# Decoder block in float32 on one core: attention outputs in token rows scaled behind the product, gate row and mask in the single-pass format, delta rule with its products grouped by shape

## The reference, cut to what matters

```
# first attention, 16 heads of 64, query blocks of 128 (k up to the block's end)
s = q @ k.T * scale + logf_cum[q] - logf_cum[k]        # "gate row"
s = where(q >= k, s, -inf)                             # mask
o = softmax(s) @ v
# second attention, 8 heads: all 256 tokens lie in one block
l = q @ k.T * scale + rel_bias[bucket(q - k)]; masked; o = softmax(l) @ v
# delta rule, 8 heads of 64, chunks of 64 tokens
decay = exp(where(causal, g_cum[i] - g_cum[j], -inf))
m     = where(strict, (k * beta) @ k.T * decay, 0)
uw    = triangular_solve(m + eye, [v * beta, k * beta * exp(g_cum)])
a     = (q @ k.T) * decay                              # attn_intra
for each chunk:
    v_new = u - w @ state
    o     = q_dec @ state + a @ v_new
    state = state * g_last + k_dec.T @ v_new
o = o * rsqrt(mean(o * o) + eps) * norm_w * silu(z)
# then [o_att, o_gdn] @ w_out
```

## Time and profile before

| | |
|---|---|
| Runs | median 1853.99 us of 3 (1853.04 to 1855.04) |
| Profiled execution | 1854.81 us, span 1852.7 us |
| Mean granted clock of PE | 0.956 |
| PE busy | 1752.1 us (95%) |
| DVE busy | 1285.6 us (69%) |
| ACT busy | 989.5 us (53%) |
| First attention, first transpose of probabilities to first output projection | 440.42 to 487.21 us |
| Second attention, to the first transpose of the delta rule | 1455.0 to 1485.39 us |
| Delta rule, to the first product of the output projection | 1485.39 to 1626.61 us |

### The profile page before, as it was taken

The page is one execution under the profiler, slowest core; times in us unless marked ns, Lnnn a source line. Parts: engine busy times, 40 slices in busy tenths (PEclk is TensorE's granted clock), DMA queues, the critical chain, the costliest instruction groups (busy, mean ns, idle before and its releaser), DMA issues. The chain is left out here.

```text
span 1852.7 us, 24961 instructions
## 1 busy us (share of the span) xinstructions
PE 1752.1 (95%) x9866; PEld 1521.5 (82%) x9866; DVE 1285.6 (69%) x1366; ACT 989.5 (53%) x1077; POOL 15.9 (1%) x21
## 2 busy tenths in 40 slices
PE   6988999899989999999999999999879898989998
PEld 5857999797778888788888888888779688969997
DVE  4954544545379888989888888989775727565554
ACT  3334334454367777767777777777545221244443
POOL 1000000000000000000000000000010000000000
PEclk9999999899979999999999999999989968889999
DMA  6405554342139898989898998989843100034550
GB/s 259 148 17 193 193 189 159 137 182 92 46 133 363 316 371 330 353 333 359 319 372 330 358 365 322 365 326 368 326 152 137 46 1 1 1 136 161 197 188 23
DMA packets 31190, 401.50 MB, mean 217 GB/s; under 512 B 3688, under 2 KB 3952, under 8 KB 5520
## 3 DMA queue, kind: packets, MB, share of 16 engines
q1 hardware_dynamic: 30704, 399.44, 57.2%
q0 software_dynamic: 416, 1.06, 0.2%
HBM read 399.43 MB, written 1.06 MB: 216 GB/s over the span
## 5 line engine op out<-in xcount | busy, mean ns | idle before, releaser
L860 DVE TENSOR_TENSOR wl<-raw,wh 128x2048 fp32r<-128x2048 f32 x266 | 607.9, 2291 | 91.8 <-ACT wh L855 88.5
L855 ACT ACTIVATE wh<-raw 128x2048 fp32r<-128x2048 f32 x264 | 506.4, 1919 | 201.6 <-PE ps L1793 90.9
L1791 PE MATMUL ps<-wh,f_r 128*128 128x512 f32 (+1 forms) x1200 | 460.3, 384 | 10.0 <-DVE wl L860 6.4
L1792 PE MATMUL ps<-wl,f_r 128*128 128x512 f32 (+1 forms) x1200 | 454.6, 379 | 0.0
L1793 PE MATMUL ps<-wh,f_r 128*128 128x512 f32 (+1 forms) x1136 | 430.2, 379 | 0.0
L1791 PEld LDWEIGHTS ps<-wh,f_r 128*128 128x128 f32 x1200 | 226.6, 189 | 54.6 <-DVE wl L860 9.6
L1792 PEld LDWEIGHTS ps<-wl,f_r 128*128 128x128 f32 x1200 | 226.7, 189 | 40.7
L1793 PEld LDWEIGHTS ps<-wh,f_r 128*128 128x128 f32 x1136 | 214.3, 189 | 40.3
L1791 PE MATMUL ps<-ht_t_r,wh 128*128 128x256 f32 x832 | 239.4, 288 | 6.2 <-DVEq L642 3.4
L1793 PE MATMUL ps<-ht_t_r,wl 128*128 128x256 f32 x832 | 238.0, 286 | 0.0
L1792 PE MATMUL ps<-h_t_r,wh 128*128 128x256 f32 x832 | 236.9, 285 | 0.0
(11 more groups left out here) (390 smaller groups left out, 2115.9 us busy)
## 6 DMA issues: line engine op xcount, KB each, us to landing
raw<-in_ws SPq DMA_DIRECT2D x169, 2048.0 KB, 8.3
raw<-in_ws SPq DMA_DIRECT2D x25, 1024.0 KB, 5.2
ring<-in_ws SPq DMA_DIRECT2D x6, 2048.0 KB, 11.2
gb<-in_gains SPq DMA_DIRECT2D x5, 512.0 KB, 8.6
x_t<-in_x SPq DMA_DIRECT2D x1, 1024.0 KB, 4.9
f<-scratch POOLq DMA_DIRECT2D x8, 128.0 KB, 3.1
out<-x_t SPq DMA_DIRECT2D x2, 512.0 KB, 2.6
cst<-in_const SPq DMA_DIRECT2D x1, 964.5 KB, 6.7
```

The costliest lines, as they stand in the source:

```text
L855: nc.scalar.activation(half_of(wh, h % SPLIT), raw_half(h % HALVES), ACT.Copy).then_inc(S("high"), 1)
L860: nc.vector.tensor_tensor(half_of(wl, h % SPLIT), raw_half(h % HALVES), half_of(wh, h % SPLIT).bitcast(F32), ALU.subtract).then_inc(S("spl ...
L1791: first = nc.tensor.matmul(bank, xh, h, start=start, stop=False)
L1792: nc.tensor.matmul(bank, xh, l, start=False, stop=False)
```

## The change

Four things are changed.

1. **First attention.** The gate row and the mask are added in the single-pass format: the row is split once into `NLH` and `NLL`, each covers both blocks with one product of 384 columns, and the mask is one product of 256 columns.
2. **Both attentions.** Probabilities are no longer divided. O is produced in token rows, four heads to a bank (weights are now the probabilities, 128 columns, and v is the moving operand, 64 columns), and DVE multiplies by the reciprocal sums when it takes the bank out. In the first attention PE transposes these rows afterwards (`heads_in_rows`, bank OT), ACT and DVE make the high and low halves, and DVE copies every other PT bank. In the second the transposes come much later, as MAT.
3. **Delta rule.** The block mask is one single-pass product of 512 columns for four heads, and the decay rows are products of 128 rows out of a zero padded `GTP`. DT, KK, C0 and QK are reordered on PE and on DVE. The last level leaves XZ out. `outputs` becomes `inside` (one product of 128 rows for each head and tile) and `from_states`.
4. **Norm after the delta rule.** `norm_w` is multiplied into `ZS` early, the squares move to ACT, and the two tiles are normed one after the other straight from PSUM. Two `high_post` move ahead.

```diff
@@ plan_attention
-                if h >= 3 and h % 2 == 1:
-                    B.add(("O", a, (h - 3) // 2))
+                if h >= 3 and (h - 3) % 4 == 0:
+                    B.add(("O", a, (h - 3) // 4))
+                if a == 0 and h >= 8 and h % 4 == 0:
+                    B.add(("OT", (h - 8) // 4))
...
@@ attention_act
-                    if h >= 2:
-                        act.wait_ge(S("probs"), n - 1)
+                    if h >= 2:
+                        filled(act, B, ("PT", a, h - 2))
...
@@ attention_dve
-                if 1 <= h <= heads:
...
-                    ch(nc.vector.reciprocal(rt[:, m + 16:m + 18], rt[:, m + 2:m + 4]))
-                    ch.go(nc.vector.tensor_scalar(PR[:, g % 2, 0:256], PR[:, g % 2, 0:256], rt[:, m + 16:m + 17], None, ALU.mult))
-                    ch(nc.vector.tensor_scalar(PR[:, g % 2, 256:384], PR[:, g % 2, 256:384], rt[:, m + 17:m + 18], None, ALU.mult))
-                    dve.sem_inc(S("probs"), 1)
...
+                if a == 0 and 2 <= h <= heads + 1 and h % 2:
+                    bank = filled(dve, B, ("PT", a, h - 2))
+                    ins = nc.vector.tensor_copy(PTS[a][:, 1, :], bank[:, 0:384])
...
+                    ch(nc.vector.reciprocal(group, group))
+                    bank = filled(dve, B, ("O", a, n))
+                    four = OTS[a][:, :, 4 * n * DH:4 * (n + 1) * DH].rearrange("p t (h d) -> p t h d", d=DH)
+                    ins = nc.vector.tensor_tensor(four, bank[:, :].rearrange("p (t h d) -> p t h d", t=TT, d=DH),
+                                                  group.unsqueeze(3).to_broadcast([P, TT, 4, DH]), ALU.mult)
...
@@ attention_pe
+                        if a == 0:
+                            pay(nc.tensor.matmul(bank[:, 0:256], qs[:, h, P:2 * P], KT[:, h // 2, 0:256], start=True, stop=False))
+                            nc.tensor.matmul(bank[:, 256:384], qs[:, h, 0:P], KT[:, h // 2, 0:P], start=False, stop=False)
+                            for part in (NLH, NLL):
+                                nc.tensor.matmul(bank[:, 0:384], IDA[:, h:h + 1].to_broadcast([P, P]), part, start=False, stop=False)
+                            ins = nc.tensor.matmul(bank[:, P:384].rearrange("p (b s) -> p b s", s=P), IDA,
+                                                   CAU.unsqueeze(1).to_broadcast([P, 2, P]), start=False, stop=True)
...
+                        nc.tensor.matmul(o[0], PT[:, g % 2, 256:384], v[0], start=True, stop=True)
+                        nc.tensor.matmul(o[1], PT[:, g % 2, 0:P], v[0], start=True, stop=False)
+                        ins = nc.tensor.matmul(o[1], PT[:, g % 2, P:256], v[1], start=False, stop=True)
...
@@ before the output projection of the first attention, then of the second
-            pe.wait_ge(S("att_done"), 1)
...
-            pe.wait_ge(S("att_done"), 2)
@@ decays
-                    for h in range(4):
-                        o = bank[:, h * P:(h + 1) * P]
-                        nc.tensor.matmul(o, ident[0:GH, 4 * q + h:4 * q + h + 1].to_broadcast([GH, P]), GTR[:, tt * P:(tt + 1) * P],
-                                         start=True, stop=False)
-                        ins = nc.tensor.matmul(o, ident, C("blockdecay"), start=False, stop=True)
+                    nc.tensor.matmul(bank[:, :].rearrange("p (h s) -> p h s", s=P), IDR, BDR.unsqueeze(1).to_broadcast([P, 4, P]),
+                                     start=True, stop=False)
+                    for h in range(4):
+                        ins = nc.tensor.matmul(bank[:, h * P:(h + 1) * P], ident[:, 4 * q + h:4 * q + h + 1].to_broadcast([P, P]),
+                                               GTP[:, tt * P:(tt + 1) * P], start=False, stop=h == 3)
...
@@ last level
-                        for n in ("XZ", "ZW"):
+                        for n in ("XZ", "ZW") if lv < LEVELS - 1 else ("ZW",):
...
@@ outputs
-                for h in range(GH):
-                    cols = slice(h * DH, (h + 1) * DH)
-                    for half in range(2):
...
+            def inside(tt):
+                bank = opened(pe, post, ("o", tt))
+                for h in range(GH):
+                    nc.tensor.matmul(bank[:, h * DH:(h + 1) * DH], ATG[:, tt, h, :], UW[:, tt, h, 0:DH], start=h == 0, stop=h == GH - 1)
...
+            for j in range(2):
+                heads_in_rows(post, ("MAT", j), 1, j, HEADS // 4)
+            inside(0)
+            next_state(1)
+            inside(1)
+            next_state(2)
+            from_states(0)
+            evacuated(("ST", 2))
+            from_states(1)
...
@@ delta_dve, behind glog
+            ch(nc.vector.tensor_tensor(heads(ZS), heads(ZS), row[:, R_NORM:R_NORM + DH].unsqueeze(1).unsqueeze(1).to_broadcast([P, TT, GH, DH]),
+                                       ALU.mult))
```

More of the change, by code:

```diff
@@ L293, in build @@
         for tt in range(TT):
+            for n in ("DT", "KK"):
+                for q in range(2):
+                    post.add((n, tt, q))
+        for n, tt in (("C0", 0), ("QK", 0), ("QK", 1), ("C0", 1)):
             for q in range(2):
[L295 to L300, removed]
+                post.add((n, tt, q))
         for lv in range(1, LEVELS):
@@ L318, in build @@
                 post.add(("QA", tt, q))
+        for j in range(2):
+            post.add(("MAT", j))
+        post.add(("o", 0))
         post.add(("ST", 1))
-        post.add(("o", 0))
+        post.add(("o", 1))
         post.add(("ST", 2))
-        post.add(("o", 1))
         plan_four(post, "mix")
@@ L583, in _ @@
                 pool.dma_start(HKBS[h // 4][:, h % 4, :], src).then_inc(S("hk_in"), 16)
+            filled(pool, post, ("ab",))
+            nc.gpsimd.memset(GTP, 0.0).then_inc(S("pad"), 1)
         def norm_act(act, B, u, ready, order, gains):
@@ L812, in attention_act, with heads_out @@
             PR, PT = PRS[a], PTS[a]
+            def heads_out(n):
+                bank = filled(act, B, ("OT", n))
+                nc.scalar.activation(HTK.hi[:, 2 * n:2 * n + 2], bank[:, :].rearrange("p (c t s) -> p c t s", t=TT, s=P),
+                                     ACT.Copy).then_inc(S("o_high"), 1)
             for h in range(heads + 3):
-                if 2 <= h <= heads + 1:
+                if 2 <= h <= heads + 1 and (a or h % 2 == 0):
                     bank = filled(act, B, ("PT", a, h - 2))
@@ L1425, in scan_dve, with decayed @@
                         let_go(post, (n, tt, q), ins)
-            for tt in range(TT):
+            def decayed(n, tt):
                 for q in range(2):
@@ L1467, in scan_dve @@
                 masked(tt, 1)
+            decayed("KK", 0)
+            begin(0)
+            decayed("KK", 1)
+            inverse_of_pairs(0)
+            begin(1)
+            decayed("QK", 0)
+            inverse_of_pairs(1)
+            decayed("QK", 1)
+            for c in (1, 2):
+                gl = GLAST[0:DH, c, :].unsqueeze(2).to_broadcast([DH, GH, DH])
+                unit = cst[0:DH, CONST["ident"]:CONST["ident"] + DH].unsqueeze(1).to_broadcast([DH, GH, DH])
+                nc.vector.tensor_tensor(GI[c], unit, gl, ALU.mult).then_inc(S("gi_ready"), 1)
             for lv in range(1, LEVELS):
@@ L2239, in _ @@
                     closed(post, ("C0", tt, q), ins)
+            pe.wait_ge(S("nar_high"), 5)
+            for tt in range(TT):
+                decays(tt)
+                transposed_out(tt, ("KT", "KBT"))
+                within("KK", tt, KBTt[tt])
+            first_level(0)
+            for tt in range(TT):
+                transposed_out(tt, ("QT", "QDT"))
+                within("QK", tt, QTt[tt])
+            first_level(1)
             for lv in range(1, LEVELS):
```

242 lines of the change are left out of this document (139 added, 103 removed).

## The result

The changed kernel takes 1800.51 us (median of 4 runs, 1798.34 to 1803.72) beside 1854.14 for the kernel before (1853.04 to 1855.04): ratio 0.971, 95% interval 0.970 to 0.973, so 53.6 us less; the forecast was 1796. The profiled execution is the longest of the four, 1803.7 us, its span 50.8 shorter than that of before.

What follows compares the result with a forecast made beforehand. PE, busy 95% of the span, was taken as the limit, in the second attention the loop through DVE. Seven terms sum to 57.8 us off 1854.8: 1797.0, as a median 1796; own range 1788 to 1804, wide range 1786 to 1811.

Steps and rivals of the forecast that it cites:

- First attention: Up to the output projection: shorter S and O make the step 2.4 us, 0.68 less over 13 steps; 6.5 us saved.
- the two pauses: First attention, S of heads 11 and 15: PE waits for a bank of O filled one step before, 0.9 lost twice.
- Weights into ZS: Ahead of the cumulative gates: one DVE product of 1024 columns that nothing hides, 1.2 us lost.
- Second attention: 30.4 us becomes 21.7, with steps up to PE's 2.43 and 2 us added for DVE; 8.7 us saved.
- Decays to level 1: End of transposes to first XZ: 51.9 us becomes 23.2, one fall of the clock included; 28.7 us saved.
- rival 1: Clock stays at 1.2 GHz through decays, KK, QK and Z, 34.6 us instead of 23.2; total 1808; chance 0.14.
- Last level: XZ for both tiles left out: 32 instructions, 3.57 us, of which 3.5 count as saved.
- Outputs and norm: Outputs, 20.5 us before, save 10.5 at full clock; norm up to the delta half of the projection, 16.4 to 15.3, saves 1.1.
- 2: Rival: O with exchanged operands costs 0.2 us an instruction, in attentions and outputs; 16 us more, total 1810; chance 0.06.
- 4: Rival: single-pass rows in the first attention's S don't pay, each costs 0.17 us more; 8 us, total 1804; chance 0.05.
- 3: Rival: handovers bind in the attentions, each group of four heads holds PE 1.1 to 1.5 us more; total 1804; chance 0.10.
- 5: Rival: slower than before, clock stays at 1.2 GHz in the levels, 100 us instead of 50; total 1868; chance 0.02.

Runs made afterwards that it cites:

- e7_division_first: Changed kernel, but probabilities divided head by head before they are transposed, as in the kernel before, with O only copied; 1820.92 us, ratio 0.983.
- e4: Changed kernel with decay products alternating for each head between gate and float32 mask, both on 128 rows; 1801.97 us, ratio 0.972.
- e5: Changed kernel with the single-pass mask first, but the four gate products behind it on 8 rows instead of the zero-padded 128; 1808.93 us, ratio 0.976.
- e10_before_128rows: Kernel before with one edit: the decays' gate product over 128 rows instead of 8; 1833.31 us beside 1852.94, ratio 0.990.
- e0_after_again: Changed kernel run once more, unedited; 1803.01 us, ratio 0.972.
- e8_wide_narrow: Changed kernel with the router's 8 moving columns repeated to 64 and the delta rule gates' 16 to 128; 1794.14 us, ratio 0.969.
- e3: Changed kernel with the decay products of before, gate on 8 rows alternating with float32 mask on 128 for each head; 1819.42 us, ratio 0.982.
- e6_old_order: Changed kernel's decay products in the order of the steps of before on PE and DVE; 1808.24 us, ratio 0.976.
- e2_old_outputs: Changed kernel with the order and shapes of the outputs of before, 112 instructions instead of 80; 1813.36 us, ratio 0.978.

## Why the prediction came out right, point by point

*First attention.* 9.3 saved, 6.5 forecast. The first transposes start 1.4 earlier (0.7 forecast; 0.6 of it lies ahead of the first S, in parts not edited), and from there to the projection it is 7.9 less (46.8 to 38.9; 5.8 forecast). The step is 2.12 + 0.11 instead of 2.4, 0.17 less in 13 steps: 2.2. The term was mis-sized above all in PT, 0.33 and not 0.42; that this comes from O behind it, which has 128 weight columns now, was not tested. S is 1.18 instead of 1.20, O 0.62 instead of 0.66, its instructions 0.11 apart as assumed. Of the two pauses each is 0.86, the forecast's 0.9. That DVE keeps up only because the division was moved, which e7_division_first shows, was in no term, though it decides the sign.

*Weights into ZS.* PE's wait 2.40 instead of 1.25: 1.15 lost, 1.2 forecast. The mean clock of the whole stretch was better, 0.91 instead of 0.83, so it shows 0.5 saved.

*Second attention.* 10.1, 8.7 forecast: the 2 us added for DVE were too many. But it is DVE that sets the pace, not PE with its 2.43: in the chain its row maxima and scalings follow each other with gaps under 0.5 us, and its row maxima start 2.1 to 2.3 us apart (1457.63, 1459.93, 1462.04).

*Decays to level 1.* 23.2 as forecast, the clock's one fall at the second tile's Z included (3.78 us for 16 instructions). But the reason given for the clock in rival 1 ("the alternation that spaced the instructions before the fall is gone") is the step that failed: 128 rows alternating keep the clock (e4), 8 rows grouped don't (e5). The forecast of this stretch was right because the change does both, which is partly luck. Of the transposes it was right: 7 us of them at 1.00, and the decays behind them too; in e10_before_128rows the clock even came back from 0.50 to 1.00 at 1488.3, among transposes that had begun at 1485.6. The rule that they don't count as work for the clock gate (The Trainium skill, TensorE: Matmul & The Clock Gate, Part 4) does not hold here.

*Last level.* 2.4, 3.5 forecast; the clock is low until 1504.8 in the first block, which takes 8.33 instead of 7.15. *Outputs and norm.* 11.0 and 1.5, 10.5 and 1.1 forecast.

*What was missing.* 12.9 us in parts not edited. 2.9 of them are PE's wait for bank 0 ahead of the MLP: the prediction looked at the order of banks in the first attention only and not at who holds a bank further on. The rest, about 10 us, stands where the clock is low, behind narrow products and waits. It repeated in the same kernel (e0_after_again). Between kernels whose earlier work begins some us sooner or later the low stretch at the gates' products was 3, 7 or 10 us, while the 32 router products, 3.98 us before, took 6.8 in every other kernel that kept eight columns. Why a shift by a few us changes it was not settled; that wider products shorten two of these places is shown (e8_wide_narrow). So the total lay in the forecast's own range by two errors of opposite sign, +5.9 and -12.9 in the trace: the near hit of the sum (1796 beside 1800.5) is luck, the parts are the evidence.

Rivals: 1 did not come in the changed kernel, and came in e5; 2 and 4 are refuted by the steps of 2.07 and 2.12; 3 by PE's waits, 3.7 us in 38.9; 5 by the levels' 47.6.

## What to carry to other kernels

Before the order of small products is tuned, look at their shape: here a product on 8 rows or with 8 to 16 moving columns took PE as long as one with 128, and the clock fell, or stayed low, among such products; padding with zeros or repeated columns cost PE nothing and was worth 19.6 us (e10_before_128rows) and 9 (e8_wide_narrow). Forecast an edit by stretches and check it by stretches: totals here hid several us in parts that nobody edited. Where a short step is bought on one engine, price the engine behind it first. And where an edit adds or drops a bank, follow the round to its end: here it cost 2.9 us some 25 us behind the last thing edited.

## What the runs showed of the hardware that was not expected

- Decay banks with the gate products on 8 rows: granted clock 0.50 for 24 us with PE busy 24.00 of them (e5_decays_8rows_grouped); with the same instructions on 128 rows, in the changed kernel, 1.00 until PE waits at 1498. The Trainium skill (TensorE: Matmul & The Clock Gate, Part 1) has the clock fall for want of activity and names gaps between products as what to avoid; here there is no gap.
- 48 products of 16 moving columns: the clock falls 3 us after the first of them and is low for 10 us (0.52 in the window, PE busy throughout); with 128 columns it stays at 1.00 (e8_wide_narrow).
- A product between neighbours with another number of rows takes 0.415 instead of 0.22 us at full clock (e3, e4). The Trainium skill (TensorEngine Tiling (Array Packing), Key Properties) says that changing the tiling mode drains the engine; if that is what happens here, these runs give the price. It is 0.2 us between 8 and 128 rows, and as much behind the KK and QK products on 64 rows (the mask product takes 0.42 there and 0.24 at first, e6_old_order, full clock); by the estimate from e2_old_outputs it is 0.06 between 128 and 64 rows where both have 64 columns.
- Two profiled executions of one kernel agreed within 0.5 us at every start compared, and in all but one of the low stretches of the clock (3.4 and 6.8 us at the first attention's start).
